# The up matrices of most experts loaded from ScalarE's DMA queue instead of SyncE's, in a two-layer mixture-of-experts decoder

## What is computed

```python
def expert_block(args):
    xb, e = args
    h = jax.nn.silu(xb @ w_gate[e]) * (xb @ w_up[e])
    return h @ w_down[e]
```

## Time and profile before

| | |
|---|---|
| median of 3 executions | 1161.84 us (1160.35 to 1163.07) |
| the profiled execution, its own time | 1160.42 us |
| its span, first to last instruction | 1158.6 us |
| TensorE busy | 837.3 us, 72% of the span |
| ScalarE busy | 152.3 us, 13% |
| VectorE busy | 154.4 us, 13% |
| moved by DMA | 438.08 MB, 378 GB/s over the span |
| mean granted TensorE clock | 0.867 of full speed |

### The profile page before, as it was taken

The page is one execution under the profiler, slowest core; times in us unless marked ns, Lnnn a source line. Parts: engine busy times, 40 slices in busy tenths (PEclk is TensorE's granted clock), DMA queues, the critical chain, the costliest instruction groups (busy, mean ns, idle before and its releaser), DMA issues.

```text
span 1158.6 us, 13913 instructions
## 1 busy us (share of the span) xinstructions
PE 837.3 (72%) x5890; PEld 435.9 (38%) x5890; DVE 154.4 (13%) x418; ACT 152.3 (13%) x338; POOL 67.9 (6%) x86
## 2 busy tenths in 40 slices
PE   9999999575656474838699899855656464656497
PEld 8555684141313131303354576332312121221235
DVE  1142431000000000000014534100000000000002
ACT  2245131000000000000010344000000000000001
POOL 0010120000000000000001542000000000000000
PEclk9999999796869696969799999987778878787898
DMA  9942758999999999999999457999999999999993
GB/s 378 421 188 77 290 218 360 428 427 427 428 429 425 428 430 427 426 430 429 426 425 421 172 198 290 424 429 427 429 427 425 430 427 429 427 428 428 428 428 142
DMA packets 37089, 438.08 MB, mean 378 GB/s; under 512 B 4144, under 2 KB 5168, under 8 KB 10288
## 3 DMA queue, kind: packets, MB, share of 16 engines
q1 hardware_dynamic: 36464, 434.92, 89.6%
q10 hardware_dynamic: 576, 2.44, 0.5%
HBM read 436.30 MB, written 1.05 MB: 377 GB/s over the span
## 4 chain that ended last, share of the span: by engine, by line
PE 44%; DMA 43%; issue 6%; DVE 2%; SPq 2%; POOL 1%; ACT 1%; POOLq 0%; DVEq 0%; ACTq 0%
PE bank L1147 19%; DMA ring<-in_w_up 9%; PE bank L874 8%; DMA arena<-in_w_up 8%; DMA ring<-in_w_down 7%; DMA arena<-in_w_gate 7%; DMA ring<-in_w_gate 7%; DMA arena<-in_w_down 5%; PE bank L1020 4%; PE bank L910 2%; SPq L414 2%; PE bank L1288 1%; PE bank L853 1%; PE bank L1100 1%; PE bank L882 1%
## 5 line engine op out<-in xcount | busy, mean ns | idle before, releaser
L1147 PE MATMUL bank<-ring,hg 128*32 128x512 f32 x1792 | 291.7, 708 | 267.6 <-DMA arena<-in_w_gate 74.4
L1147 PEld LDWEIGHTS bank<-ring,hg 128*32 128x32 f32 x1792 | 77.0, 127 | 455.2 <-issue 364.3
L1147 PE MATMUL bank<-arena,hg 128*32 128x512 f32 x256 | 141.0, 714 | 0.0
L1147 PE MATMUL bank<-ring,arena 128*32 128x512 f32 x704 | 105.7, 630 | 29.6 <-DMA ring<-in_w_down 16.9
L874 PE MATMUL bank<-ring,hg 128*128 128x512 f32 x224 | 98.9, 595 | 0.0
L1648 DVE TENSOR_TENSOR arena<-arena,bank 128x512 f32<-128x512 f32 x16 | 11.0, 688 | 541.0 <-PE bank L1147 541.0
L1020 PE MATMUL bank<-arena,ring 128*128 128x256 f32 x256 | 64.1, 388 | 1.4 <-ACT arena L822 1.4
L1147 PEld LDWEIGHTS bank<-ring,arena 128*32 128x32 f32 x704 | 29.1, 115 | 88.7 <-issue 75.5
L1147 PE MATMUL bank<-arena 128*32 128x512 f32 x192 | 59.8, 613 | 1.4 <-ACT arena L733 1.4
L874 PEld LDWEIGHTS bank<-ring,hg 128*128 128x128 f32 x224 | 41.7, 190 | 49.0 <-issue 48.5
L1100 PEld LDWEIGHTS bank<-arena,hr 128*128 128x128 f32 x448 | 51.1, 192 | 11.7 <-issue 11.7
(11 more groups left out here) (206 smaller groups left out, 664.3 us busy)
## 6 DMA issues: line engine op xcount, KB each, us to landing
ring<-in_w_up SPq DMA_DIRECT2D x56, 2048.0 KB, 21.7
ring<-in_w_gate SPq DMA_DIRECT2D x50, 2048.0 KB, 20.1
ring<-in_w_down SPq DMA_DIRECT2D x48, 2048.0 KB, 20.3
arena<-in_w_down SPq DMA_DIRECT2D x8, 2048.0 KB, 10.1
arena<-in_w_up SPq DMA_DIRECT2D x8, 2048.0 KB, 29.3
arena<-in_w_gate SPq DMA_DIRECT2D x8, 2048.0 KB, 27.6
ring<-w_ab SPq DMA_DIRECT2D x6, 2048.0 KB, 30.9
arena<-in_w_down SPq DMA_DIRECT2D x12, 1024.0 KB, 27.0
```

Of the source, the lines that this page charges most:

```text
L1147: op = pe.matmul(dst[rows, :], lhsT[:, q, rows], unit[s][:, q, cols], start=(q == 0), stop=(q == steps - 1))
```

## The change

The four up matrices of quads 2 to 7 are no longer issued by SP but by ACT, in a new function `load_ups` that ACT calls between `copy_weights` and `silu`. It waits for the same semaphore value, 3i. SP's loop leaves them out (j = 4 to 7) and goes from the gates of a quad to its downs. The ACT loop is written over two quads at a time, since slots alternate between even and odd quads; quads 1 and 2 come before it and the last behind it. Nothing is computed differently, and the same bytes go to the same slots.

```diff
--- before.py
+++ after.py
@@ -393,17 +393,17 @@
             off = (head % 2) * HD
             return t[off:off + HD, head // 2 if chunk is None else chunk, :]
 
+        def expert_unit(l, e, kind):
+            one = bass.ds(e, 1)
+            if kind < 2:
+                return (w_gate, w_up)[kind][l, one].rearrange("a (p k) n -> p (a k) n", k=KD)
+            return w_down[l, one].rearrange("a (p m) n -> p (a m) n", m=MH)
+
         block = ctx.enter_context(nc.Block())
 
 
         @block.sync
         def _(sp):
-            def expert_unit(l, e, kind):
-                one = bass.ds(e, 1)
-                if kind < 2:
-                    return (w_gate, w_up)[kind][l, one].rearrange("a (p k) n -> p (a k) n", k=KD)
-                return w_down[l, one].rearrange("a (p m) n -> p (a m) n", m=MH)
-
             def expert_flat(l, e, kind):
                 return (w_gate, w_up, w_down)[kind][l, e].rearrange("(p k) n -> p (k n)", p=P)
 
@@ -446,7 +446,7 @@
                         sp.dma_start(slot_out(LOOP_SLOTS[l][k])[:, rows, :], expert_unit(l, e, 2)[:, rows, :]).then_inc(landed, 16)
 
                 def quad(i, which):
-                    for j in range(QUAD_UNITS):
+                    for j in (*range(QUAD), *range(2 * QUAD, QUAD_UNITS)):
                         e = (i % QUADS) * QUAD + j % QUAD
                         sp.compute_val(e * (D * DE) * 4)
                         if j % QUAD == 0:
@@ -757,14 +757,34 @@
                 act.wait_ge(once["rounds"], l + 1)
                 last = act.value_load(rounds[0:1, l, 1:2], min_val=QUADS - 1, max_val=QUADS * PASSES - 1)
                 n = act.value_load(rounds[0:1, l, 0:1], min_val=QUADS, max_val=QUADS * PASSES)
-                with act.Fori(1, last) as i:
+                half = act.value_load(rounds[0:1, l, 3:4], min_val=QUADS // 2 - 1, max_val=QUADS * PASSES // 2 - 1)
+
+                def load_ups(i, which):
+
+                    act.wait_ge(m["used"], 3 * i)
+                    for j in range(QUAD, 2 * QUAD):
+                        e = (i % QUADS) * QUAD + j % QUAD
+                        act.compute_val(e * (D * DE) * 4)
+                        k = ring_place((which, 0), j)[0]
+                        act.dma_start(slot_in(LOOP_SLOTS[l][k]), expert_unit(l, e, 1)).then_inc(m["landed"][k], 16)
+
+                def middle(i, which=None):
                     copy_high(i)
                     copy_weights(i)
+                    if which is not None:
+                        load_ups(i, which)
                     silu(i)
                     take_high(i + 1)
                     copy_hidden(i)
+
+                middle(1)
+                middle(2, 1)
+                with act.Fori(1, half) as t:
+                    middle(2 * t + 1, 0)
+                    middle(2 * t + 2, 1)
                 copy_high(last)
                 copy_weights(last)
+                load_ups(last, 0)
                 silu(last)
                 act.wait_ge(m["pickT"], n)
                 for pair in range(2):
```

## The result

The changed kernel took 1182.34 us, the median of 6 executions (1176.73 to 1186.14), against 1160.73 for the kernel before in 6 executions. The ratio is 1.0181, with a 95% interval of 1.0161 to 1.0202. The forecast was 1183, range 1168 to 1203.

What follows compares the result with a forecast made beforehand. The DMA rate was taken as the bound. Late last gates 7.0 plus idle time 3.5 make 10.5 us per layer, 21.0 for two; on 1160.4 that is 1181.4, plus 1.4 for the median: 1183 us, range 1168 to 1203.

Steps and rivals of the forecast that it cites:

- The gates come late by what is left of them, doubled: Every round: ups share the rate equally, so the 7.0 us of gates left take 14.0 and come 7.0 us late.
- In the last quads it is paid in full: Last quad of each layer: TensorE no longer waits for loads after the gates, so their 7.0 us delay counts once per layer.
- the bound: Long-end case with downs product 7.07 us, gates 10.0: 7.8 us of gates left, 2.0 us idle per round, 1197 us.
- Idle time: Quads 2 to 6: DMA engines have nothing queued for 0.7 us per round, 3.5 us per layer.
- First byte 0.9 us after the issue: Ups on ScalarE's queue and downs on SP's: the first byte moves 0.9 us after the issue.
- my 2.8 us: Every load: from its last byte to TensorE's start pass 2.8 us.
- Turns of whole transfers: Rival: each engine finishes its part of a 2 MB load before changing queue; gates 4.9 us late, 1172 us; chance 0.12.
- No change: Rival: gates keep precedence, ups are delayed inside an existing wait; 1162 us; chance 0.08, including late issues on ACT.
- Faster: Rival: two queues keep 431 GB/s in the loops instead of 427.5; 6 us less, 1156 us; chance 0.03.
- ScalarE's issues taken up late: Rival: ups start later, each microsecond taking about one off the gates' delay; chance counted within no change's 0.08.
- TensorE slow throughout its gates: Rival: after longer waits all 16 gate steps run at 0.85, gates take 13.7 us; 1233 us; chance 0.06, shared with larger ups share.

Runs made afterwards that it cites:

- One matrix: Kernel before, with only the fourth up matrix of each of quads 2 to 7 issued by ScalarE, the other three by SyncE: 1176.28 us.
- two gave the same as four: Kernel before, with the third and fourth up matrices of quads 2 to 7 issued by ScalarE, the first two by SyncE: 1181.51 us.
- The two complementary runs: Changed kernel with quad 7's ups back on SyncE, 1165.38 us; and with only quad 7's ups on ScalarE, 1178.54 us.
- the moved `combine`: Changed kernel with the last quad's sum and turned weights put in front of its gates product on TensorE: 1172.30 us.
- the run with the ups behind the fourth gate matrix: Changed kernel, but ScalarE issues the ups only when the fourth gate matrix of the same quad has landed: 1249.0 us.
- the gates, in whole loads: Gates of quads 2 to 7 on ScalarE's queue instead of the ups, odd quads' last down matrix as one DMA: 1167.11 us, ratio 1.0046.

## Why the prediction was right, and which of its steps were off

*The gates come late by what is left of them, doubled.* Right in kind. I had 7.0 us; the mean over twelve rounds is 26.4 - 19.5 = 6.9. That it fits so well is in part luck, as two errors behind it offset one another (below, at the first byte). One matrix gave 4.8 for 4.9, two gave the same as four.

*In the last quads it is paid in full.* Right, and a little larger: 8.0 in both layers, since both times the downs' product took the shorter 7.07 us, for which the bound had 7.8. The two complementary runs and the moved `combine` show where it is paid.

*Idle time.* Right in kind, too large in size. I had 3.5 us per layer; the table has 2.7 and 0.8. It does not come in every round either. The rate between the downs of quad 1 and those of quad 6 fell from 428 to 423 GB/s in layer 0 and to 422 in layer 1; why the same fall lengthened layer 1's rounds by 0.8 us only was not taken apart.

*First byte 0.9 us after the issue.* Wrong where it was used. The row is an issue into empty queues. In the changed kernel the four ups are issued at 549.45, and the DMA view from 549.5 to 552.5 us shows SP's queue alone:

```profile
q1 hardware_dynamic: 83, 1.26, 98.6%
```

The first packet on q10 starts at 552.97, 3.5 us behind the issue, and in all twelve rounds of this profile it is 3.4 to 3.6. That is not ScalarE's queue being slow in itself: in the run with the ups behind the fourth gate matrix, ScalarE issues into empty queues, and there the first packet comes 1.0 to 1.1 us behind the issue in all twelve rounds (587.08 and 588.11 in layer 0's last). So the engines' work on the other queue makes the difference. It leaves fewer bytes of gates to share. From 553 us on, when the ups do move, the gates have 2.69 MB left, 6.3 us:

```profile
q10 hardware_dynamic: 457, 6.73, 71.9%
q1 hardware_dynamic: 196, 2.69, 28.7%
```

Doubled they end at 565.6, and with my 2.8 us TensorE would start at 568.4; it started at 569.44. A microsecond more than 2.8 thus passed between the gates' computed last byte and TensorE's start. The 16 DMA engines are not equally far: behind 565.6 SP's queue still has, up to 569.4,

```profile
q1 hardware_dynamic: 19, 0.11, 7.2%
```

and its last packet of gates ends at 568.25, 1.2 us before TensorE starts. That sharing doubles their distance would explain the extra microsecond; this is argued, not shown. For this round the bound had 7.8 us of gates left; 6.3 were, and the gates still came 8.0 late, by 6.3, this 1.0, and 0.7 that stay open.

*The passage between the layers.* Not in the prediction at all: 4.9 us. Of it 1.7 us are a longer stall of TensorE in layer 0's last quad, at the output of the third expert: in the profile after the step is 6.4 us (606.26 to 612.64), before 4.7 (596.62 to 601.33).

```profile
608.19 1.13 PE L1232 MATMUL bank<-hg 32*128 32x256 f32 x12
610.93 0.70 PE L1232 MATMUL bank<-hg 32*128 32x256 f32 x4 [1.60 <-issue]
```

It waits there for nothing that the profile names. In the run with only the last quad on two queues the stall is 2.59 us. Another 1.6 us come at the start of layer 1's mixer, which does the same work at a lower granted clock, 0.83 where it had been 1.00 (first after, then before):

```profile
663.00:673.00 10.00, 8.87 (x40) 5.42 (x41) 6.12 (x14) 1.71 (x6) 7.91 (x9) 0.83 0.43 160
```

```profile
651.00:660.00 9.00, 7.17 (x40) 4.57 (x41) 5.50 (x16) 2.06 (x8) 7.43 (x9) 1.00 0.43 155
```

And 1.3 us come at the gates of layer 1's quad 1, for which TensorE waits 3.60 us instead of 2.33 (760.52 and 746.32). What the stall is, and what lies behind these two, stays open. The term that was too large (7.0 of idle time against 3.5) and this one that was missing cancelled in part: the sum 21.0 for 23.4 in the profiles and 21.6 in the medians is better than its parts, and that is luck. The late last gates, 16.0 of the 23.4, are the part that was forecast with its reason.

*The rivals.* Turns of whole transfers: excluded by both queues moving from the start of the sharing, 62 packets beside 55 in 4 us. "No change" was excluded by the same rows. The rule on the turns (the Trainium skill, "DMA: Bandwidth & Descriptors", section "Queues, rings and completion order": round robin, a packet at a time, typically 9 to 17 descriptors) agrees with the runs in that the queues take turns. In the length of a turn it does not: with its typical packet, an engine's eight rows of a load would have gone in one turn, and here a turn was one row of 16 or 8 KB. The measurement decides. Faster: the windows of the changed loop give 423 to 426 GB/s, none above the 427 to 428 of before. ScalarE's issues taken up late: the 3.5 us are this rival's delay, though it came from busy engines and not from ScalarE; in layer 0's last round it left 6.3 us of gates to share where the bound had 7.8. TensorE slow throughout its gates: they took 8.4 to 10.0 us, no longer than before, although they started after 14.7 to 20.2 us of waiting.

*What was said to show it.* Gates about 27 us behind the downs (24.3 to 27.6), ups some 12 behind the gates (11.5 to 16.6, on average 13.3), waits before the gates near 19 (14.7 to 20.2), before the ups 2 to 3 (2.3 to 7.6), the loop at 422 to 424 GB/s (423 over 380 us; the two windows of the earlier trace rows give 425 and 426).

## What to carry to other kernels

Where the DMA engines are the bound, one queue in the order of use lets the transfer that is needed next have the whole rate. Moving part of the stream to a second queue added no bandwidth here and made a load late by what moved beside it, up to its own remainder; the middle of the loop hid most of that, the last round, behind which only compute is left, paid for it. How much it costs depends on which loads are moved: the gates, in whole loads, cost 0.5% where the ups cost 1.8%. When two queues can't be avoided, look at both pairs that will meet, not only at the first, and at the row sizes, since they decide who gets more.

## What the runs showed of the hardware that I had not expected

- Two queues take turns by rows, not by bytes: 75 packets beside 72, with 1.15 and 0.59 MB, when the rows are 16 and 8 KB. Halving a transfer's rows halved its weight. For one down matrix in every second quad this was worth 17 us (1184.14 against 1167.11).
- An issue on one queue while the other kept the DMA engines busy took 3.4 to 3.6 us to its first packet, against 1.0 to 1.1 for the same queue when both were empty.
- Behind a wait of 2.65 us half a product took 8.71 us, against 7.06 for the half before it without a wait, the granted clock being 0.63 in its first 4.5 us and 1.00 in the other half. Work that had filled the gap was not waste: moving it away cost 0.2%.
- The changed kernel's executions spread over 0.8% (1176.73 to 1186.14) where those of before spread over 0.3%. The gates' delay goes with how long the downs' product took in that round: the gates start on average 27.3 us behind the downs where that was 7.07 us, and 25.5 where it was 8.4 to 9.9. The one-queue order hides this; that it makes the spread is a conjecture.
